# A MoE expert stage with its up-projection bias seeded into PSUM by ScalarE in place of bias products on TensorE

## The reference, cut to what matters

```python
h = xb @ w_up[e] + b_up[e]
g = jnp.minimum(h[:, :D_FF], SWIGLU_LIMIT)
lin = jnp.clip(h[:, D_FF:], -SWIGLU_LIMIT, SWIGLU_LIMIT)
act = g * jax.nn.sigmoid(SWIGLU_ALPHA * g) * (lin + 1.0)
return act @ w_down[e] + b_down[e]
```

## Time and profile before

| | us |
|---|---|
| median of three runs | 2248.12 |
| the runs | 2245.98 to 2250.63 |
| the profiled execution: its span | 2239.1 |
| the profiled execution's own time | not listed; the median lies 9.0 above the span |
| mixer and routing, 0 to 560 | 560 |
| 34 passes, with what starts and ends them, 560 to 2221 | 1661 |
| final norm and stores, 2221 to 2239.1 | 18.1 |

### The profile page before, as it was taken

The page is one execution under the profiler, slowest core; times in us unless marked ns, Lnnn a source line. Parts: engine busy times, 40 slices in busy tenths (PEclk is TensorE's granted clock), DMA queues, the critical chain, the costliest instruction groups (busy, mean ns, idle before and its releaser), DMA issues.

```text
span 2239.1 us, 32629 instructions
## 1 busy us (share of the span) xinstructions
PE 2147.8 (96%) x10498; PEld 1784.5 (80%) x10499; DVE 1606.1 (72%) x1842; ACT 1206.7 (54%) x1239; POOL 559.1 (25%) x519
## 2 busy tenths in 40 slices
PE   7999988997899999999999999999999999999996
PEld 7887987685687888888888888888888888888885
DVE  4788876458855656787588675977975787677766
ACT  4422261331744545566476565757754676565755
POOL 1001031115301112124044041414411252121313
PEclk9999999997999999999999999999999999999998
DMA  7224276413966766889599695979986799778877
GB/s 185 64 79 142 81 163 205 167 67 138 360 218 218 229 212 220 305 282 353 184 363 369 231 324 181 376 268 302 369 289 213 250 365 328 226 246 295 296 248 270
DMA packets 287302, 541.65 MB, mean 242 GB/s; under 512 B 37302, under 2 KB 53798, under 8 KB 286146
## 3 DMA queue, kind: packets, MB, share of 16 engines
q1 hardware_dynamic: 262866, 495.07, 63.7%
q0 software_dynamic: 24368, 45.72, 8.1%
HBM read 513.61 MB, written 65.13 MB: 258 GB/s over the span
## 4 chain that ended last, share of the span: by engine, by line
PE 58%; issue 6%; DVE 6%; ACT 3%; DMA 2%; DVEq 0%; ACTq 0%; POOL 0%; SPq 0%; POOLq 0%
PE ex_ps_l L2927 8%; PE ex_ps_l L2926 8%; PE ex_ps_g L2926 7%; PE ex_ps_g L2927 7%; PE ex_ps_y L2926 5%; PE ex_ps_y L2927 5%; PE ex_ps_g L2930 4%; PE ex_ps_l L2930 4%; PE ex_ps_y L2930 3%; DVE ex_w_lo L2693 3%; PE ex_ps_t L2864 2%; ACT ex_w_hi L2561 2%; PE ex_ps_t L2874 2%; PE ex_ps_l L2881 1%; PE ex_ps_g L2936 1%
## 5 line engine op out<-in xcount | busy, mean ns | idle before, releaser
L2693 DVE TENSOR_TENSOR ex_w_lo<-ex_late,ex_w_hi 128x2048 fp32r<-128x2048 f32 x204 | 464.0, 2289 | 230.9 <-ACT ex_w_hi L2561 166.9
L2401 POOL TENSOR_TENSOR ex_passed<-keep_ident 128x1 f32<-128x1 f32 x136 | 137.0, 1007 | 1153.3 <-ACT ex_y L2604 1126.5
L2561 ACT CAST ex_w_hi<-ex_late 128x2048 fp32r<-128x2048 f32 x170 | 324.6, 1909 | 129.4 <-PE ex_ps_g L2927 62.8
L2693 DVE TENSOR_TENSOR ex_w_lo<-keep_sig_o,ex_w_hi 128x2048 fp32r<-128x2048 f32 x136 | 310.1, 2291 | 111.1 <-ACT ex_w_hi L2561 111.1
L2561 ACT CAST ex_w_hi<-keep_sig_o 128x2048 fp32r<-128x2048 f32 x134 | 255.2, 1905 | 136.0 <-PE ex_ps_g L2927 39.1
L2926 PE MATMUL ex_ps_g<-ex_w_hi,ex_x_hi 128*128 128x512 f32 x784 | 308.2, 393 | 3.3 <-DVE ex_w_lo L2693 1.8
L2926 PE MATMUL ex_ps_l<-ex_w_hi,ex_x_hi 128*128 128x512 f32 x784 | 308.9, 394 | 1.2 <-DVE ex_w_lo L2693 1.2
L2927 PE MATMUL ex_ps_g<-ex_w_lo,ex_x_hi 128*128 128x512 f32 x784 | 306.6, 391 | 0.0
L2927 PE MATMUL ex_ps_l<-ex_w_lo,ex_x_hi 128*128 128x512 f32 x784 | 305.9, 390 | 0.0
L2926 PE MATMUL ex_ps_y<-ex_w_hi,ex_h_hi 128*128 128x512 f32 x544 | 217.8, 400 | 3.1 <-DVE ex_h_lo L2729 2.5
L2930 PE MATMUL ex_ps_g<-ex_w_hi,ex_x_lo 128*128 128x512 f32 x544 | 212.7, 391 | 0.0
(11 more groups left out here) (502 smaller groups left out, 4081.2 us busy)
## 6 DMA issues: line engine op xcount, KB each, us to landing
keep_sig_o<-in_w_up_dram SPq DMA_DIRECT2D x102, 1024.0 KB, 8.8
ex_late<-in_w_up_dram SPq DMA_DIRECT2D x102, 1024.0 KB, 8.8
ex_late<-in_w_down_dram SPq DMA_DIRECT2D x102, 1024.0 KB, 8.1
keep_weights<-in_w_up_dram SPq DMA_DIRECT2D x68, 1024.0 KB, 8.3
keep_sig_o<-in_w_down_dram SPq DMA_DIRECT2D x34, 1024.0 KB, 8.1
st_tab<-tabs SPq DMA_DIRECT2D x8, 1408.0 KB, 11.8
keep_weights<-in_w_in_dram SPq DMA_DIRECT2D x5, 1024.0 KB, 5.5
pr_late_pieces<-in_w_in_dram SPq DMA_DIRECT2D x5, 1024.0 KB
```

The costliest lines, as they stand in the source:

```text
L2401: pool.tensor_tensor(passed[:, :], ident[:, 0:1], ident[:, 0:1], ALU.add).then_inc(passed_done, 1)
L2561: nc.scalar.copy(w_hi[:, j % SPLIT, :, :], raw(j)).then_inc(hi_done, 1)
L2693: v.tensor_tensor(w_lo[:, j % SPLIT, :, :], raw(j), w_hi[:, j % SPLIT, :, :].bitcast(F32), ALU.subtract).then_inc(lo_done, 1)
```

## The change

The bias products go, with `pick`, `row_pick`, `bias_hl`, `bias_rows` and the VectorE copies. Instead ScalarE issues one DMA per pass that fetches the expert's bias row to all 128 partitions (`load_bias`, 128 x 2048 floats, 1 MiB in SBUF), as soon as the seeds of the pass that used the tile before are done. ScalarE then copies quarters of this tile into the PSUM banks ahead of the products (`seed_g`, `seed_l`; the latter adds 1), and all products accumulate onto them. In a pair's half-filled second block the seeds of the upper 64 rows are multiplied by 0 (`one_above`). The first gate bank of a pass is seeded in the pass before (`seed_first`, at j = 10). TensorE waits for the seeds at j = 0, 2, 4 and 6. The four products of the start, which went into ps_g[0], go one into each of the four banks.

```diff
-        bias_hl = sb("bias_hl", [P, 2 * F], F32R)
+        bias = sb("bias", [P, 2 * F], F32)
...
-                for i in range(2):
-                    sp.dma_start(bias_rows[i * E:(i + 1) * E, :], p["b_up"][0]).then_inc(bias_in, 16)
...
+                pool.memset(one[:, :], 1.0).then_inc(ones_set, 1)
+                pool.memset(one_above[0:SMALL, :], 1.0).then_inc(ones_set, 1)
+                pool.wait_ge(ones_set, 2)
+                pool.memset(one_above[SMALL:P, :], 0.0).then_inc(ones_set, 1)
...
-                pool.memset(bias_hl[2 * E:P, :].bitcast(F32), 0.0).then_inc(bias_zeroed, 1)
...
+                def load_bias(e):
+                    act.dma_start(bias[:, :], p["b_up"][0][bass.ds(e, 1), :].to_broadcast([P, 2 * F])).then_inc(bias_in, 16)
+
+                def load_next_bias(n, e_next):
+                    act.wait_ge(l_seeded, n * 2 + 2)
+                    load_bias(e_next)
+
+                def seed_g(bank, half, above=False):
+                    scale = one_above[:, 0:1] if above else 1.0
+                    return nc.scalar.activation(bank[:, :], bias[:, half * 512:half * 512 + 512], ACT.Copy, scale=scale)
+
+                def seed_l(bank, half, above=False):
+                    plus = one_above[:, 0:1] if above else one[:, 0:1]
+                    scale = one_above[:, 0:1] if above else 1.0
+                    return nc.scalar.activation(bank[:, :], bias[:, F + half * 512:F + half * 512 + 512], ACT.Identity,
+                                                bias=plus, scale=scale)
+
+                def seed_first(n):
+                    act.wait_ge(bias_in, n * 16 + 16)
+                    seed_g(ps_g[0], 0).then_inc(g_first_seeded, 1)
...
+                    if blocks == 2:
+                        act.wait_ge(glu_done, n * 10)
+                        seed_g(ps_g[1], 0, small).then_inc(g_seeded, 1)
+                    if kind is not ALONE:
                         hi(n, SPLIT - 1, True)
+                    act.wait_ge(lin_read, n * 4)
+                    act.wait_ge(y_b_read, n + 1)
+                    if blocks == 2:
+                        seed_l(ps_l[0], 0)
+                        seed_l(ps_l[1], 0, small).then_inc(l_seeded, 1)
+                    else:
+                        seed_l(ps_l[0], 0).then_inc(l_seeded, 1)
+                        act.wait_ge(glu_done, n * 10)
+                        seed_g(ps_g[1], 1).then_inc(g_seeded, 2)
+                        seed_l(ps_l[1], 1).then_inc(l_seeded, 1)
+                        if kind is AHEAD:
+                            load_next_bias(n, e_next)
                     for j in range(CHUNKS):
+                        if blocks == 2 and j == 2:
+                            act.wait_ge(glu_done, n * 10 + 3)
+                            seed_g(ps_g[0], 1)
+                            seed_g(ps_g[1], 1, small).then_inc(g_seeded, 1)
+                        if blocks == 2 and j == 4:
+                            act.wait_ge(lin_read, n * 4 + 2)
+                            seed_l(ps_l[0], 1)
+                            seed_l(ps_l[1], 1, small).then_inc(l_seeded, 1)
+                            if kind is AHEAD:
+                                load_next_bias(n, e_next)
...
+                        if kind is AHEAD and j == 10:
+                            act.wait_ge(glu_done, n * 10 + 7)
+                            seed_first(n + 1)
...
-                    if j == 0 and first_part:
-                        pe.wait_ge(pick_set, n + 1)
+                    if j == 0:
+                        if first_part:
+                            pe.wait_ge(g_first_seeded, n + 1)
+                        else:
+                            pe.wait_ge(g_seeded, n * 2 + 1)
+                    elif j == 4:
+                        pe.wait_ge(g_seeded, n * 2 + 2)
+                    elif j in (2, 6):
+                        pe.wait_ge(l_seeded, n * 2 + (j // 4 + 1))
...
-                            first = kk == 0
+                            first = kk == 0 and not up
...
-                            col = (j // 2) % 2 * F + (j // 4) * 512
-                            mm = pe.matmul(to[:, :], pick[:, b, :], bias_hl[:, col:col + 512], start=False, stop=True)
```

More of the change, by code:

```diff
@@ L2141, in experts @@
         x_lo = sb("x_lo", [P, PAIR, KD, P], F32R)
-        pick = sb("pick", [P, 2, P], F32R)
+        one = sb("one", [P, 1], F32)
+        one_above = sb("one_above", [P, 1], F32)
         places, ident, nowhere, x_rows = keep["places"], keep["ident"], keep["nowhere"], keep["x_rows"]
-        bias_rows = sb("bias_rows", [P, 2 * F], F32)
+        end_rows = sb("end_rows", [P, 2, D], F32)
         gather_at = sb("gather_at", [P, PAIR], U32)
@@ L2621, in square_row, with item @@
                                          accum_out=row_mean[:, b:b + 1]).then_inc(row_squared, 1)
-                def item(n, kind, blocks, small=False):
+                def item(n, kind, blocks, e_next, small=False):
                     if kind is not ALONE:
@@ L2662, in _ @@
                                    ps_t[half][:, :].rearrange("p (k t) -> p k t", k=4)).then_inc(t_hi, 1)
-                act.wait_ge(h3_out, 16 * TT)
-                act.wait_ge(bias_plus, 1)
-                nc.scalar.copy(bias_hl[0:2 * E, :], bias_rows[0:2 * E, :]).then_inc(bias_hi_set, 1)
+                act.wait_ge(primed, 1)
+                act.wait_ge(ones_set, 3)
+                seed_first(0)
                 hi(0, 2, False)
                 def one_pass(n, e, blocks, plan, kind=AHEAD, small=False):
-                    item(act.snap(n), kind, blocks, small)
+                    e_next = e + 1 - single_follows(e, plan) if blocks == 2 else e + 1
+                    item(act.snap(n), kind, blocks, e_next, small)
                 with act.Fori(0, E - 1) as e:
@@ L2679, in later @@
                         x_high(n, ALONE, blocks, b, x_turn_no(ALONE, b))
-                    item(n, ALONE, blocks)
+                    act.wait_ge(glu_done, n * 10)
+                    seed_first(n)
+                    item(n, ALONE, blocks, None)
                 def norm_again():
@@ L2694, in lo, with x_low @@
                                     w_hi[:, j % SPLIT, :, :].bitcast(F32), ALU.subtract).then_inc(lo_done, 1)
-                def choose_second(e, small):
-                    rows = SMALL if small else P
-                    v.tensor_copy(pick[:, 1, 0:rows], keep["row_pick"][:, bass.ds(e, 1)].to_broadcast([P, rows]))
-                    if small:
-                        v.memset(pick[:, 1, SMALL:P].bitcast(F32), 0.0)
-                def x_low(n, kind, blocks, b, i, e=None, small=False):
+                def x_low(n, kind, blocks, b, i, small=False):
                     for half in range(2):
-                        if b and half:
-                            choose_second(e, small)
                         v.wait_ge(t_hi, turned(n, kind, blocks, i + half))
@@ L2838, in later @@
                     for b in range(blocks):
[L2839 to L2840 removed]
+                        x_low(n, ALONE, blocks, b, x_turn_no(ALONE, b))
+                    item(n, ALONE, blocks)
                 def norm_again():
@@ L2880, in low_rows @@
                     for k in range(4):
-                        pe.matmul(to[:, :], lo_in[:, b, 4 * part + k, :], w_hi[:, s, k, :], start=False, stop=False)
+                        pe.matmul(to[:, :], lo_in[:, b, 4 * part + k, :], w_hi[:, s, k, :], start=False, stop=False,
+                                  skip_group_check=True)
                 def multiply(n, kind, j, blocks, full, mine):
@@ L2916, in multiply @@
                             kk = 4 * part + k
-                            first = kk == 0
-                            last = (not up) and part == 1 and k == 3
+                            first = kk == 0 and not up
+                            last = part == 1 and k == 3
                             if b and k == 3:
@@ L2925, in multiply @@
                                         low_rows(to, lo_in, b, part, s)
[L2926 removed]
+                            pe.matmul(to[:, :], hi_in[:, b, kk, :], w_hi[:, s, k, :], start=first, stop=False,
+                                      skip_group_check=True)
                             mm = pe.matmul(to[:, :], hi_in[:, b, kk, :], w_lo[:, s, k, :], start=False,
[L2928 removed]
+                                           stop=last and b > 0, skip_group_check=True)
                             if b == 0:
[L2930 to L2936 removed]
+                                mm = pe.matmul(to[:, :], lo_in[:, b, kk, :], w_hi[:, s, k, :], start=False, stop=last,
+                                               skip_group_check=True)
                     if mine[-1] == blocks - 1:
@@ L2953, in item @@
                             x_turn(n, kind, blocks, 0, next_turn_no(blocks))
-                for _ in range(4):
-                    pe.matmul(ps_g[0][:, :].rearrange("p (a n) -> p a n", a=4), ident[:, :],
```

(5 more changed lines are left out.)

65 lines of the change are left out of this document (16 added, 49 removed).

## The result

The changed kernel takes 2266.05 us (median of 4 runs, 2264.69 to 2267.98), the kernel before 2247.16 us beside it: ratio 1.0077, 95% interval 1.0064 to 1.0089. By the ratio it is slower by 17 us; the forecast said 8.3.

A forecast was written before the change was run, and what follows sets the result against it. TensorE was taken to bound the expert part, with DMA also full in one-block passes. Pairs' products -27.2, loads +31.3 and ScalarE's head +4.2 gave +8.3 on 2239.1, 2247.4; plus 9.0 to the median, 2256 us, range 2236 to 2280.

The forecast's parts named there:

- the case named likeliest: Whole kernel: slower by 8.3 us, about 2256 us, own range 2250 to 2265; chance 0.45.
- The products of pairs, -27.2: Two-block passes: 120 bias products removed from TensorE, 8 in each of 15 passes, save 27.2 us.
- TensorE at 68.1 us in full pairs and some 57.5 in half-filled ones: Sign expected in the profile after: two-block passes shorten from 69.9 and 59 to 60 us.
- The cover that it named: Two-block passes: slower use of chunks hides the bias load; without it each load would cost 2.8 us.
- The loads, +31.3: DMA in one-block and first passes: bias loads of 1 MiB, 2.78 us each, not hidden there, add 31.3 us.
- That 1.04 is full: One-block passes: a DMA share of 1.04, at 372 to 377 GB/s, means the engines have no room left.
- ScalarE's head, +4.2: Start of six passes after half-filled pairs: late seeds make TensorE wait, +0.7 us each, +4.2 us together.
- It waits 1.6 us and has 0.9 us fewer products: +0.7 us: One pass after a half-filled pair: TensorE's wait for the first ps_l seed less products saved, net +0.7 us.
- it just fits: Steady one-block pass: seed and fifth chunk arrive in time, with 0.9 and 0.6 us to spare.
- TensorE's 17.3 us buy nothing: One-block passes: removing 76 bias products, 17.3 us, gains nothing, as DMA sets the pace.
- Much slower: Rival: loads at 3.5 us cost 11 us more, ScalarE's late head delaying VectorE 8 more; 2275 us, chance 0.15.
- What would show it: Profile signs: shorter pairs, one-block passes at 36.9 to 39 us, ScalarE load waits of tens of us, TensorE waiting on w_lo.

The follow-up runs named there:

- e4: The kernel before plus one unread 1 MiB broadcast load of a bias row per pass from ScalarE's queue; 2275.12 us, ratio 1.0140.
- e1: The changed kernel with the bias row loaded once before the first pass and never again; 2228.11 us, ratio 0.9931.
- e3: The changed kernel with the bias row loaded only once and every seed one column wide instead of 512; 2208.70 us, ratio 0.9843.
- e5: The changed kernel with the first ps_l seed moved ahead of the cast of weight chunk 3 in one-block passes; ratio 1.0076.
- e7: The changed kernel with the next pass's bias row sent to 64 partitions instead of 128, 0.5 MiB a pass; ratio 1.0053.

## Why the prediction was right, and where its size was off

Direction and range held (2266 in 2236 to 2280, slower at 0.60). The mechanism of the case named likeliest held too, but 2266 lies just above the 2250 to 2265 that it gave itself. The size did not hold: +17.3 us by the ratio, against +8.3. By its own terms:

- **The products of pairs, -27.2**: measured -26.3. "TensorE at 68.1 us in full pairs and some 57.5 in half-filled ones" came out at 68.1 and 57.3. The cover that it named, the slower use of chunks, holds the loads too: pairs in e4 are unchanged.
- **The loads, +31.3**: measured +31.5 in e4. The price of 2.78 us a load was 2.7, and its split by runs held in part: +19.8 for the three runs of three is 18.6, with +6.6 for the one at 1113.9 us of the earlier trace rows at 6.5; the first pass's +4.2 is 3.8, the lone pass's +1.0 behind a full pair is 0.9, and the 0 of the three behind half-filled ones is 0.1. But the runs of two paid 9.6 instead of 6.3, and the last pass 2.3 instead of 0. So the passes of that execution add up to 35.8, and that the total by the ratio lies within 0.2 us of the forecast is in part luck. Two reasons were given for a share above 1, overlap of two queues and waiting inside packets; no run here separates them. That 1.04 is full, on which the sum rests, is borne out. By the Trainium skill (DMA: Bandwidth & Descriptors, Rules for kernel authors) a second issuing engine brings no bandwidth; e4 agrees: with both queues running, no pass of it is above 387 GB/s. The 425 GB/s of its section Measured, by which the load would have been free, wasn't reached in any run here.
- **ScalarE's head, +4.2: the step that failed, by size.** What is left is 17.3 + 26.3 - 31.5 = 12.1 us, and e1 shows it alone: 26.2 - 15.5 = 10.7 by the ratio, 12.9 by its passes. Of these, 9.6 us are in the five passes behind half-filled pairs and 1.7 in the last, the six for which the forecast had 4.2; 4.3 are in the other one-block passes, for which it had none; the first pass is 2.7 shorter.
  "It waits 1.6 us and has 0.9 us fewer products: +0.7 us" took the first seed as the only wait. That wait was 1.8 us, about as forecast, but these passes paid 1.9 us each. ScalarE is full there, so its delay comes back at chunk 8, where TensorE waits 1.07 us in e1 and 0.13 before: 1.8 + 0.9 - 0.9 for the products is 1.8, near the 1.9.

```profile
1297.27 0.50 PE L2956 MATMUL ex_ps_y<-ex_w_hi,ex_h_hi 128*128 128x512 f32 x1 [1.07 <-DVE ex_h_lo L2765]
```

  For the steady state, "it just fits" held at both places that it named: in the second pass of e1's run of three TensorE waits neither for the seed nor for the fifth chunk. But it waits 0.74 us at chunk 8 for h_lo, where it had no wait before:

```profile
1163.74 0.50 PE L2956 MATMUL ex_ps_y<-ex_w_hi,ex_h_hi 128*128 128x512 f32 x1 [0.74 <-DVE ex_h_lo L2765]
```

  VectorE starts on the fifth chunk 7.7 us into this pass instead of 6.2, and from there to that h_lo it has no gap. With this, the passes behind another one-block pass are 0.4 us longer than before, though they have four products less: 3.1 us in eight. Those behind a full pair are 1.2 over in four.
- **"TensorE's 17.3 us buy nothing" in one-block passes**: nearly so. With neither loads nor wide seeds (e3) they give 2 to 7 of the 17, and the seeds take that back.
- **Much slower**, 2275 us, had a dearer load and ScalarE's late head in it. Its first half did not happen; its second half, ScalarE delaying VectorE's chain in one-block passes, is what was missing from the sum: it was put at 8 us, and what e1 has above the 4.2 is 6.5 us by the ratio and 8.7 by its passes. The case as a whole had a chance of 0.15.
- **What would show it**: ScalarE waits for loads for 52 us, and seven of the 17 one-block passes between the first and the last are near or within "36.9 to 39 us" (36.8 to 38.4), but the last of each run (39.7 to 41.6) and those behind a half-filled pair (39.7 to 40.5) are beyond. "TensorE waiting on VectorE's w_lo" became a wait on h_lo at chunk 8.

The reading of the chain alone would mislead. TensorE's longest waits are put down to VectorE's h_lo, its wait behind half-filled pairs to a seed (in e1; to "issue" in the change); moving that seed gave nothing (e5), since behind the one wait stood another of the same engine.

## What to carry to other kernels

Before moving work to an engine with idle time, look for the stretch in which it has none: 640 us free over the expert part did not help in a stretch of 13 us without a gap, and there each added operation is paid in full, wherever it is put. Price such additions per kind of pass, and keep the change to the passes that have room: the same idea with the one-block passes left alone and only half of a pair's biases seeded (h2) turned 17 us of loss into 9 of gain. Costs on two full resources overlap, so take them away both singly and together before giving each its share.

## What was unexpected of the hardware

- A broadcast of an 8 KB row to 64 partitions took 2.1 us of all 16 DMA engines by the time of its packets, one to 128 partitions 2.7 us: half the bytes, 78% of the time (e7).
- An operand that is a tile adds 0.08 us to ScalarE's 128x512 copy: 0.60 us with none, 0.69 and 0.70 with one, 0.77 with two. Writing PSUM from SBUF (0.603) was about as quick as the reverse (0.586 for 64 rows, 0.611 for 128 in the earlier trace rows). The Trainium skill (ScalarE: Activation LUTs, Step-by-step) calls PSUM the faster destination; source and destination both differ between these rows, so they neither bear that out nor refute it.
- After waits of 3.0 us and more in the middle of a one-block pass, and after some shorter ones, TensorE's granted clock fell to 1.2 GHz for 3.4 us. The kernel before has no such wait and no such fall from its fourth pass to its last.
